# Gate and up weights laid out by chunk, hidden activations turned by VectorE, rows beyond 64 in two blocks of 32

## The reference, cut to what matters

```python
def swiglu(h, wg, wu, wd):
    return (jax.nn.silu(h @ wg) * (h @ wu)) @ wd

def moe_swiglu(h, w_router, wg, wu, wd):
    t = h.reshape(-1, shp[-1])
    logits = (t @ w_router).astype(F32)
    top_v, top_i = lax.top_k(logits, TOP_K)
    gates = jax.nn.softmax(top_v, axis=-1)
    out = jnp.zeros_like(t)
    for e in range(N_EXPERTS):
        w_e = jnp.sum(jnp.where(top_i == e, gates, 0.0), axis=-1).astype(t.dtype)
        out = out + w_e[:, None] * swiglu(t, wg[e], wu[e], wd[e])
    return out.reshape(shp)
```

## Time and profile before

| | us |
|---|---|
| median of three runs | 1920.5 |
| profiled execution | 1920.83 |
| its span, first to last instruction | 1918.9 |
| experts' stage: first weight load issued | 996.0 |
| experts' stage: first gate and up product | 1042.8 |
| TensorE busy | 1799.5 (94%) |
| VectorE busy | 740.7 (39%) |
| ScalarE busy | 483.4 (25%) |

### The profile page before, as it was taken

How to read it: one execution, slowest core, us unless ns; L and a number is a source line. 1 busy time by engine, 2 the same in 40 slices (tenths; PEclk the granted TensorE clock), 3 DMA queues, 4 the chain that set the end, 5 groups by cost and what they waited for, 6 DMA issues and landing times.

```text
span 1918.9 us, 23057 instructions
## 1 busy us (share of the span) xinstructions
PE 1799.5 (94%) x9605; PEld 1076.3 (56%) x9606; DVE 740.7 (39%) x1263; ACT 483.4 (25%) x810; POOL 412.9 (22%) x233
## 2 busy tenths in 40 slices
PE   5999988989999999899888999999999999987886
PEld 2777557868788888798554343333433334332332
DVE  4864865656634344630453222111411104111323
ACT  4343256642222222432352101111010110110111
POOL 1531561433444334354630000000000000000000
PEclk9999998999999999999999999999999999998998
DMA  9344000234555531355328999999989998999996
GB/s 368 136 182 188 19 1 2 89 132 133 197 190 204 200 152 66 131 89 153 99 84 340 415 410 410 401 391 387 403 333 384 389 409 319 413 414 411 410 413 253
DMA packets 154870, 485.43 MB, mean 253 GB/s; under 512 B 26512, under 2 KB 53569, under 8 KB 143485
## 3 DMA queue, kind: packets, MB, share of 16 engines
q1 hardware_dynamic: 154296, 483.02, 66.1%
q10 hardware_dynamic: 453, 0.65, 0.1%
HBM read 482.57 MB, written 1.07 MB: 252 GB/s over the span
## 4 chain that ended last, share of the span: by engine, by line
PE 65%; DMA 6%; DVE 4%; SPq 2%; issue 1%; ACT 1%; POOL 0%; DVEq 0%; ACTq 0%; POOLq 0%
PE PS L2813 22%; PE PS L2830 10%; PE PS L2612 5%; PE PS L2613 5%; PE PS L2616 5%; DMA BIG<-in_od_exp_wu 4%; PE PS L2204 3%; PE PS L2205 3%; PE PS L2206 3%; PE PS L2774 1%; PE PS L2730 1%; DMA BIG<-in_od_exp_wg 1%; PE PS L2804 1%; DMA QB<-in_od_exp_wg 1%; PE PS L2784 1%
## 5 line engine op out<-in xcount | busy, mean ns | idle before, releaser
L2813 PE MATMUL PS<-BIG,QB 128*64 128x448 f32 x1344 | 265.1, 551 | 17.2 <-DMA BIG<-in_od_exp_wu 10.9
L766 POOL TENSOR_TENSOR BIG_parts<-BIG,QB_parts 128x2048 fp32r<-128x2048 f32 x33 | 156.4, 4740 | 230.1 <-ACT QB_parts L934 229.9
L2813 PEld LDWEIGHTS PS<-BIG,QB 128*64 128x64 f32 x1344 | 96.3, 139 | 176.7 <-issue 175.4
L2830 PE MATMUL PS<-BIG,ZS 128*64 128x512 f32 x840 | 184.7, 593 | 2.5 <-ACT ZS L1343 2.5
L2813 PE MATMUL PS<-BIG,HB 128*64 128x448 f32 x800 | 156.5, 547 | 5.9 <-issue 5.9
L766 POOL TENSOR_TENSOR BIG_parts<-BIG,BIG_parts 128x2048 fp32r<-128x2048 f32 (+1 forms) x25 | 114.6, 4585 | 150.5 <-ACT BIG_parts L934 142.2
L2612 PE MATMUL PS<-HB_parts,QB_parts 128*128 128x512 f32 (+1 forms) x384 | 140.9, 373 | 0.4 <-issue 0.4
L1343 ACT ACTIVATE ZS<-PS 128x896 f32<-128x896 f32 x32 | 29.4, 918 | 415.7 <-PE PS L2804 415.7
L2830 PEld LDWEIGHTS PS<-BIG,ZS 128*64 128x64 f32 x840 | 60.0, 137 | 118.5 <-issue 118.3
L2123 DVE TENSOR_TENSOR MOD<-QB,PS 64x448 f32<-64x448 f32 x32 | 19.7, 615 | 269.6 <-ACT QB L1337 259.7
L2813 PEld LDWEIGHTS PS<-BIG,HB 128*64 128x64 f32 x800 | 56.9, 139 | 98.6 <-issue 97.4
(11 more groups left out here) (420 smaller groups left out, 3172.8 us busy)
## 6 DMA issues: line engine op xcount, KB each, us to landing
BIG<-in_od_exp_wg SPq DMA_DIRECT2D x55, 1792.0 KB, 15.7
BIG<-in_od_exp_wu SPq DMA_DIRECT2D x55, 1792.0 KB, 18.6
BIG<-in_od_exp_wd SPq DMA_DIRECT2D x50, 1792.0 KB, 18.1
BIG<-in_ada_w SPq DMA_DIRECT2D x24, 2048.0 KB, 8.4
QB<-in_od_exp_wg SPq DMA_DIRECT2D x9, 1792.0 KB, 12.9
XT<-in_od_exp_wu SPq DMA_DIRECT2D x9, 1792.0 KB, 17.0
QB<-in_od_exp_wd SPq DMA_DIRECT2D x7, 1792.0 KB, 10.5
XT<-in_od_exp_wd SPq DMA_DIRECT2D x7, 1792.0 KB, 14.4
```

Source lines behind the costliest of these rows:

```text
L766: pool.tensor_tensor(r12(w), w, r12(high), ALU.subtract).then_inc(split_l, 1)
L2813: last = mm(PS[at:at + 64, bank, 0:GROUP], XGS[x][:, 4 * part + k, r0:r0 + 64], wgu[u][:, k, GROUP * c:GROUP * c + GROUP], start=(part + k ...
L2830: last = mm(PS[64 * n:64 * n + 64, bank, :], HET[:, s % 2, k, r0:r0 + 64], half[:, a, :], start=(k == 0), stop=(k == 6))
```

## The change

1. **Layout.** Before the launch the gate and up weights are put in the order in which the loads take them, so each load is one run of 14336 bytes per partition.
2. **Turning.** In the rounds of experts 0 to 6 VectorE turns the activations from `HE` straight to `HET` in 16 transposes of 32 rows by 224 columns (seven blocks of 32 by 32). TensorE's `columns` and ScalarE's copy stay for expert 7 alone.
3. **Rows beyond 64.** Rows 64 to 95 are multiplied if the expert has more than 64 rows, rows 96 to 127 if it has more than 96, each by `extra_rows`, for both parts at once, in blocks of 32 columns of the array. Both stand before part 1's ordinary products. In group 1 the two results of a block lie 32 partitions apart from those of group 0, so VectorE's product of the second group takes two operations of 32 rows in place of one of 64.
4. **Slots.** Since part 0's weights are needed by `extra_rows`, `gu_mm` now comes from the first product of part 1.

```diff
-            wg, wu = (A[n].rearrange("o e (b k p) n -> (o e) b p k n", b=2, p=P) for n in ("od_exp_wg", "od_exp_wu"))
+            wg, wu = A["od_exp_wg"], A["od_exp_wu"]
...
-                    src = (wg, wu)[u][e, part, :, :, 2 * GROUP * p:2 * GROUP * p + 2 * GROUP]
-                    sp.dma_start(expert_slot(at).rearrange("p (k n) -> p k n", k=4), src).then_inc(arrived_e[at], 16)
+                    sp.dma_start(expert_slot(at), (wg, wu)[u][e, part, p, :, :]).then_inc(arrived_e[at], 16)
...
-                    if s:
+                    if s and alone:
                         hidden_columns(s - 1)
...
+                for tier, rows in enumerate(EXTRA_ROWS):
+                    seq(dve.tensor_scalar(OV, CNT, float(P + rows), None, ALU.is_gt))
...
+            def hidden_columns(w, s, opening):
+
+                dve.wait_ge(e_h, NGR * w + 2 * s + 2)
+                if not (opening and s < 2):
+                    dve.wait_ge(dn_mm, 2 * NPAIR * w + max(0, 2 * s - 2))
+                for j in range(4):
+                    for i in range(4):
+                        hidden, rows = slice(32 * j, 32 * j + 32), slice(32 * i, 32 * i + 32)
+                        last = dve.transpose(HET[hidden, s % 2, :, rows],
+                                             HE[s % 2][rows, 224 * j:224 * j + 224].rearrange("p (q k) -> p k q", k=7))
+                last.then_inc(e_htev, 1)
...
-                        dve.tensor_tensor(to[64:P, :], SE[0:64, c, :], PS[0:64, 2 + c, 0:GROUP], ALU.mult)
+                        for r0, of, n in ((64, 0, 64),) if c == 0 else ((64, 32, 32), (96, 0, 32)):
+                            dve.tensor_tensor(to[r0:r0 + n, :], SE[of:of + n, c, :], PS[of:of + n, 2 + c, 0:GROUP], ALU.mult)
...
+                    if own is None:
+                        hidden_columns(w, s, opening)
                     if s:
                         take_down(w, s - 1, nx)
...
+                            if part and c + k + u == 0:
+                                last.then_inc(gu_mm, 1)
                     return last
+
+                def extra_rows(x, tier, parts):
+
+                    r0 = EXTRA_ROWS[tier]
+                    for k in range(KB):
+                        for c in range(2):
+                            for u in range(2):
+                                at = 64 - 64 * u + 32 * ((tier + c) % 2)
+                                mm(PS[at:at + 32, 2 + c, 0:GROUP], XGS[x][:, k, r0:r0 + 32],
+                                   parts[k // 4][u][:, k % 4, GROUP * c:GROUP * c + GROUP],
+                                   start=(k == 0), stop=(k == KB - 1), tile_position=(0, at))
...
-                        with pe.If(more[x] > 0):
-                            gate_up(x, 0, 1, part, wgu)
-                            if s and part == 0:
-                                pe.wait_ge(e_h, NGR * w + 2 * s)
-                            gate_up(x, 1, 1, part, wgu)
-                        last = gate_up(x, 0, 0, part, wgu)
+                        if part:
+                            with pe.If(more[x] > 0):
+                                extra_rows(x, 0, parts)
+                            with pe.If(most[x] > 0):
+                                extra_rows(x, 1, parts)
+                        last = gate_up(x, 0, part, parts[part])
...
-                        if part == 0 and s:
+                        if part == 0 and s and own:
                             columns(s - 1)
...
+def by_chunk(w):
+
+    n = FFE // (2 * GROUP)
+    blocks = np.asarray(w).reshape(E, 2, 4, P, n, 2 * GROUP)
+    return blocks.transpose(0, 1, 4, 3, 2, 5).reshape(E, 2, n, P, SLOT_E)
```

More of the change, by code:

```diff
@@ L1329, in _, with wave @@
             act.wait_ge(e_zero, 1)
-            def wave(w, nx, opening=False):
+            def wave(w, nx, opening=False, alone=False):
                 def silu(s):
@@ L1340, in hidden_columns @@
                     act.wait_ge(e_htr, NPAIR * w + s + 1)
-                    if not (opening and s < 2):
-                        act.wait_ge(dn_mm, 2 * NPAIR * w + max(0, 2 * s - 2))
+                    act.wait_ge(dn_mm, 2 * NPAIR * w + max(0, 2 * s - 2))
                     act.activation(HET[:, s % 2, :, :].rearrange("p a b -> p (a b)"),
@@ L1355, in wave @@
                     silu(2 * s + 1)
-                hidden_columns(NPAIR * nx - 1)
+                if alone:
+                    hidden_columns(NPAIR * nx - 1)
             for w, nx in ROUNDS:
@@ L1363, in _ @@
             with act.Fori(PAIRED, waves) as w:
-                wave(w, 1)
+                wave(w, 1, alone=True)
             act.nop().then_inc(done["act"], 1)
@@ L1997, in _ @@
             seq(dve.tensor_copy(CNT, PS[:, 3, 16:24]))
-            seq(dve.tensor_scalar(RFB[:, 0:E], CNT, float(P // 2), None, ALU.is_gt))
-            dve.tensor_copy(RIB[:, 0:E], RFB[:, 0:E]).then_inc(rt_ev, 1)
+            for tier, rows in enumerate(EXTRA_ROWS):
+                last = dve.tensor_scalar(RFB[:, tier, 0:E], CNT, float(rows), None, ALU.is_gt)
+            seq(last)
+            dve.tensor_copy(RIB[:, :, 0:E], RFB[:, :, 0:E]).then_inc(rt_ev, 1)
             dve.wait_ge(rt_e, 1)
@@ L2793, in _, with wave @@
             pe.nop().then_inc(e_sc, 4)
-            def wave(w, nx, more, own=False, following=False, opening=False):
+            def wave(w, nx, more, most, own=False, following=False, opening=False):
                 def columns(s):
                     pe.wait_ge(e_h, NGR * w + 2 * s + 2)
-                    if not (opening and s == 0):
-                        pe.wait_ge(e_htev, NPAIR * w + s)
+                    pe.wait_ge(e_htev, NPAIR * w + s)
                     for j in range(7):
@@ L2864, in wave @@
                             pe.wait_ge(e_gev, 4 * w + 4)
-                        gate_up(x, 1, 0, part, wgu).then_inc(e_grp if part else gu_mm, 1)
+                        last = gate_up(x, 1, part, parts[part])
+                        if part:
+                            last.then_inc(e_grp, 1)
                         if s == 0 and part and not opening:
@@ L2887, in wave @@
                     gather(1, 0, 2)
-                columns(NPAIR * nx - 1)
+                if own:
+                    columns(NPAIR * nx - 1)
                 if following:
+                    pe.wait_ge(e_h, NGR * w + 2 * NPAIR * nx)
                     gather(0, 1, 1)
@@ L2899, in _ @@
             with pe.Fori(PAIRED, waves) as w:
-                wave(w, 1, [pe.value_load(RIB[0:1, bass.ds(w, 1)], min_val=0, max_val=1)], own=True)
+                more, most = ([pe.value_load(RIB[0:1, tier, bass.ds(w, 1)], min_val=0, max_val=1)] for tier in range(2))
+                wave(w, 1, more, most, own=True)
             scatter(waves, 1, 1)
@@ L2916 @@
     nc = bacc.Bacc("TRN2", target_bir_lowering=False, num_devices=1, dynamic_dma_scratch_size=1024)
+    inputs |= {n: by_chunk(inputs[n]) for n in ("od_exp_wg", "od_exp_wu")}
     arrays, A = {}, {}
```

33 lines of the change are left out of this document (18 added, 15 removed).

## The result

The changed kernel takes 1905.03 us (median of 4 runs, 1901.12 to 1908.41) against 1920.72 us (4 runs): a ratio of 0.992, 95% interval 0.990 to 0.993. The forecast was 1880 us, within 1868 to 1905. The direction is right. The gain is 15.7 us where 40 were forecast, and the median lies at the very edge of the range, 0.03 us outside. The profiled execution took 1901.12 us (span 1899.0), the quickest of the four; its account is held against the prediction's 1880.4.

The account below looks back on a forecast made before the run. TensorE paces rounds (1, 2) and (3, 4), weight loads the rest, so the DMA's account counts: 29.8 us from layout, 19 from idle time, 8.6 given back for slots, 40.4 less in all: 1880 us, range 1868 to 1905.

Parts of the forecast that it names:

- the head of a round: Start of each round of two: add_scattered queues behind the transposes, TensorE waits 3.3 us; in (5, 6) the loads hide it.
- Turning, VectorE's side: Sixteen transposes per step on VectorE take 7.6 us, hidden in ordinary steps, with less cover at heads and ends of rounds.
- The size of a transpose: One 32 x 224 transpose on VectorE: 0.476 us from a line through two shapes, bounds 0.302 and 0.53.
- None: End of a round: TensorE's wait for VectorE costs 1 us in expert 0's round, none in (1, 2), which has no tables.
- DMA idle time above 40 us: Listed sign that the forecast is wrong: the weight loads' DMA standing idle for more than 40 us.
- Layout: Gate and up loads as one run per partition go at 428 GB/s instead of 406: 29.8 us less.
- rival 1: The layout brings nothing, 406 GB/s having another cause than run length: 1892 us; chance 0.11.
- Turning, TensorE's side: TensorE saves 1.2 us per step without the identity products: 9.2 us each in rounds (1, 2) and (3, 4), expert 0's 4.4.
- Rows beyond 64: 6.0 us per 32-row block: expert 1 runs two, 12.0 as before; expert 4 one, 24.1 us less.
- rivals 2 and 3: 2: stationary loads pace the 32-column blocks, 1893, chance 0.08; 3: blocks go two at a time, 1953, 0.08 including unseen stalls.
- Slots: Part 0's slots come back later, leaving the loads' lead two slots shorter after round (3, 4): 8.6 us lost, bounds 0 and 8.6.
- Rival 4: VectorE becomes the bound at 0.9 us per transpose, its step 18.9 us against TensorE's 18.0: 1908 to 1921; chance 0.06.

Follow-up runs that it names:

- a3: Changed kernel with add_scattered put ahead of the first step's transposes in each round of two experts; 1881.08 us, ratio 0.980.
- c1: Changed kernel with four more transposes per step on VectorE, into cells that nothing reads; 1919.21 us, ratio 1.000.
- a4: Changed kernel with the first step of each round of two and the last step of every round turned by TensorE and ScalarE; 1878.23 us, ratio 0.979.
- c4: a3 with, besides, the last step of each round of experts 0 to 6 turned by TensorE and ScalarE; 1886.29 us, ratio 0.982.
- c3: a4 with the old layout of the gate and up weights; 1895.99 us, ratio 0.988.
- b1: a4 with the 32-row blocks split by part, so part 0's slots come back after part 0; 1877.7 us, ratio 0.978.
- a2: Changed kernel with the 32-row blocks split by part, part 0's block ahead of the step's first group; 1893.29 us, ratio 0.986.
- a1: Changed kernel with part 2 (Turning) undone: TensorE and ScalarE turn every step of experts 0 to 6; 1903.71 us, ratio 0.992.
- b2: a1 with the 32-row blocks split by part, so part 0's slots come free after part 0; 1894.01 us, ratio 0.986.
- b4: Changed kernel with 36 small unread products on TensorE before its wait for add_scattered at heads of rounds of two; 1907.8 us, ratio 0.993.

## Why the prediction missed

**The step that failed** is the head of a round in *Turning, VectorE's side*: "TensorE waits 3.3 us, once per round; in (5, 6) the loads hide it", 6.6 us in the sum. Each head costs some 7.2, and none is wholly hidden: a3, which takes away the three waits and nothing else, is 24 us faster by the medians (20.0 by round in the profiled executions). c1 shows it the other way round: 2.4 us more in VectorE's queue, 14.2 us more in all. That a3 lands at 1881, on the forecast, is in part luck: the sum held 6.6 us for heads that a3 doesn't have, so by its own terms a3 should have come to some 1873. Three errors lie in that one step.
- *The size of a transpose.* 576 ns and 0.59 from start to start, where the line through the earlier trace rows gave 0.476 and the upper bound was 0.53 (in proportion). So 16 take 9.4 us and not 7.6, which turns 3.3 us of waiting (3.2 by the prediction's own times) into 5.05. This one reads every seventh float (28 bytes apart). That the stride is the reason was not tried. The text gave the slope itself (1.6 us per head for each 0.1 us), and the slope holds: 1.6 x 1.14 = 1.8, and 3.3 + 1.8 = 5.1.
- *What follows a wait.* The block behind it runs partly at the lower clock and takes 8.3 us instead of 6.2. No term stood for that. The trace of before has no such wait in these rounds (clock 1.00 throughout in the earlier trace rows), but where it waits for weights, after 1610, its clock is 0.95: the row was there to be asked.
- *"The loads hide it" in (5, 6).* a3's last stretch is 4.0 us shorter with that head gone, so only 3.2 of 7.2 were hidden.

**By round**, in the profiled execution (predicted in brackets):
- Expert 0: first product 1040.5, end 1124.1 (1125.4). The stage began 2.3 us earlier than before; the round itself took 83.6 (82.6), with 1.8 us of waits at its end (1.0).
- (1, 2): 240.9 (236.2), +4.7: 1.75 more waiting, 2.1 for the slow block, 0.5 for the selection's transposes at the lower clock (1.11 for 0.66 us); 0.3 are not placed.
- (3, 4): 223.1 (212.1), +11.0: the same 4.4; at the end 2.26 of waiting and a slower down part behind it (13.9 us in the chain instead of 12.0); 1.8 of waiting of kind C; 0.6 are not placed. "None" was claimed for the end of a round without tables. That holds in (1, 2), where 12.0 us of expert 1's second rows cover it, and not in (3, 4), where expert 3 has only 6.0.
- From there to the end of the span: 310.9 (304.8), +6.1. The head costs 4.0 of it. The end of (5, 6), 9.77 us of waiting that the prediction overlooked altogether, is mostly hidden by the loads: with the ends of (3, 4) and (5, 6) both free, the last packet comes 3 us earlier (a4 and c4 against a3).

One of the prediction's signs of being wrong came: DMA idle time above 40 us. From the first load at 993.9 to the last packet at 1879.1 are 885 us, 62 more than the 823.1 at 428 GB/s. And waits for weights began at 1675, not near 1580.

**What held.** *Layout*: 426 and 431 GB/s in mixed runs (428). Its worth depends on what else waits: 7.1 us alone, 5.9 in the change, 17.8 with the heads free; rival 1 came to 12 between 1892 and 1880, and c3 is 1896. Rival 1 itself falls with the speed. So does, here, the rule of the Trainium skill ("DMA: Bandwidth & Descriptors", Specifications) that 512 bytes are enough for the full rate: with the DMA's share at 1.00 or more, loads go at 405 and 406 GB/s in c3 and at 426 and 431 in the change. The layout changes the length of the runs and their places in DRAM together; no run tells the two apart. *Turning, TensorE's side*: the seven products and the 0.15 are gone (1.06 and 0.15 are 1.21 and not the sum's 1.15, half a us per round). *Rows beyond 64*: 6.08 and 6.15 us per block (6.0), one block for expert 4; rivals 2 and 3 fall.

*Slots*: taken as 8.6 us. With the heads free they are worth 0.5 (b1), which is within the spread of the runs; in the change at most some 6 of a2's 11.7, and that isn't shown; the 9.7 of a1 and b2 go with waits of kind C. So the forecast of 1880 held 8.6 us for something that does not stand beside free heads, and a4 still ends at 1878: in its last stretch (287.8 us, 419 GB/s against 428) some 6 us remain that no run here places.

**Rival 4** named the right engine and the wrong place. It made VectorE the bound of every step from 0.9 us per transpose on. At 0.59 its ordinary steps stay covered; the chain at a head comes due far earlier, from 0.27 on by the prediction's own numbers (3.3 us at 0.476, 1.6 per 0.1). The rule beside it ("VectorE: DVE Perf Modes", Rules for kernel authors, in the Trainium skill: a 128x128 transpose is TensorE's) is borne out only at those places: a1, with all of them on TensorE, is no faster than the change, nor is b2 than a2 (1894.0 and 1893.3, both with early slots and hardly a wait of kind C); a4, with 7 of 28 steps on TensorE, is 27 us faster than the change.

**What no term stood for** besides: waits for the program itself, 3.5 us in the profiled execution of the change and up to 23.3 in its variants. The trace of before has none, so the prediction could not read them there.

## What to carry to other kernels

When work moves to an engine with spare time, list what queues behind it at each place where the order is irregular (first and last step of a round), and let the bound on its duration go above proportion to the nearest shape. A wait of TensorE costs its length and then a slow block, so price both, here 7.2 us for a wait of 5.05. And put what another engine waits for ahead of what nobody needs yet: three lines in VectorE's program gave 24 us, the whole change 15.7. Before a variant is read as a test of a theory, look at what ends each of its waits: in a1 and b4, waits for instructions looked like waits for weights.

## What had not been expected of the hardware

- A transpose of 32 rows by 224 columns, read 28 bytes apart, takes 576 ns; 128 columns in a row take 302. That is 2.57 ns per column against 2.36 and, for 1024, 1.88.
- After 5.05 us without products the granted clock was 0.71 in the next 9 us and 1.00 behind them; with 4.4 us of small products in the wait it stayed at 1.00 at the heads of (3, 4) and (5, 6). At that of (1, 2) in b4, where 0.84 us of waiting for VectorE and 1.39 of kind C remained, it was 0.81.
- Four products in 32-column blocks, into two PSUM banks, go in the time of two in 64-column blocks: 12.16 us for 128 records, though each of their weight loads takes 110 ns as in the earlier trace rows.
- TensorE can stand still inside a step for 0.5 to 6 us with no semaphore to wait for, 2.2 to 2.6 us from the start of a 16 KB packet of instructions to the next product. In b4 such waits come to 23.3 us, in c4 to 14.5, in a4 to none.
